# Seven block products for eight in gate and up, a down projection from scratch, and attention scores in tiles of 64 by 32

## The reference, cut to what matters

```python
h = concatenate([pad, meta, x])                        # 1024 tokens and 16 meta tokens, width 1024
proj = rmsnorm(h, norm1_g) @ w_in                      # q, k, v of attention; q, f, i, g of HGRN2
o_sb = group_rmsnorm(stick_breaking_attention(q, k, v), sb_norm_g)   # 8 heads of width 64
#   z = q @ k.T * scale; w = exp(log_sigmoid(z) + sum of log_sigmoid(-z) over later keys); w @ v
o_hg = group_rmsnorm(hgrn2_chunkwise(...), hg_norm_g) * silu(hg_g)
h = h + concatenate([o_sb, o_hg]) @ w_out
u2 = rmsnorm(h, norm2_g)                               # 1024 x 1024
h = h + (silu(u2 @ w_gate) * (u2 @ w_up)) @ w_down     # w_gate, w_up: 1024 x 2816, w_down: 2816 x 1024
return rmsnorm(h, final_norm_g)
```

## Time and profile before

| | us |
|---|---|
| median of 3 runs | 1439.6 (1439.37 to 1439.84) |
| the profiled execution: time | 1441.7 |
| the profiled execution: span of the core | 1439.7 |
| PE busy in the span | 1382.0 |
| DVE busy | 738.8 |
| ACT busy | 439.2 |
| GpSimd (POOL) busy | 20.2 |

### The profile page before, as it was taken

One profiled execution on the slowest core, in us unless ns is written; L12 is line 12 of the kernel. 1 busy time (PEld: TensorE's weight loads), 2 busy tenths in 40 slices (PEclk: granted clock), 3 DMA queues, 4 the chain that ended last, 5 costly groups with the idle time before them and its releaser, 6 DMA issues.

```text
span 1439.7 us, 22130 instructions
## 1 busy us (share of the span) xinstructions
PE 1382.0 (96%) x9404; PEld 1165.2 (81%) x9404; DVE 738.8 (51%) x1180; ACT 439.2 (31%) x768; POOL 20.2 (1%) x48
## 2 busy tenths in 40 slices
PE   6999999998999999699999999999999999999998
PEld 5898989887677776499987888888888888888886
DVE  6476677763776565822633515253342525152447
ACT  6323322223665556810522211111111211121113
POOL 3000000000000000010000000000000000000000
PEclk9999999999999999999999999999999999999999
DMA  6211111110010000041021102020201102020202
GB/s 192 59 31 30 31 31 50 31 41 1 1 60 2 31 2 30 2 161 60 30 74 59 59 30 88 0 88 18 70 29 58 58 29 85 3 87 0 88 0 117
DMA packets 61199, 68.86 MB, mean 48 GB/s; under 512 B 1584, under 2 KB 54832, under 8 KB 61120
## 3 DMA queue, kind: packets, MB, share of 16 engines
q1 hardware_dynamic: 59408, 61.94, 13.2%
q0 software_dynamic: 1712, 5.78, 1.1%
HBM read 63.51 MB, written 4.19 MB: 47 GB/s over the span
## 4 chain that ended last, share of the span: by engine, by line
PE 92%; ACT 4%; DVE 2%; issue 1%; DMA 0%; ACTq 0%; DVEq 0%; POOLq 0%
PE ps L269 19%; PE ps L271 18%; PE ps L270 18%; PE ps L1552 17%; PE ps L945 3%; PE ps L281 2%; PE ps L282 2%; PE ps L283 2%; PE ps L909 2%; PE ps L551 2%; PE ps L925 2%; PE ps L386 1%; ACT bv L505 1%; PE ps L542 1%; ACT a_hi L1020 0%
## 5 line engine op out<-in xcount | busy, mean ns | idle before, releaser
L269 PE MATMUL ps<-a_hi,w_hi 128*128 128x512 f32 (+2 forms) x960 | 358.5, 373 | 8.9 <-DVE a_lo L378 2.9
L270 PE MATMUL ps<-a_lo,w_hi 128*128 128x512 f32 (+2 forms) x960 | 350.1, 365 | 0.0
L271 PE MATMUL ps<-a_hi,w_lo 128*128 128x512 f32 (+2 forms) x960 | 349.9, 364 | 0.0
L269 PEld LDWEIGHTS ps<-a_hi,w_hi 128*128 128x128 f32 x960 | 181.8, 189 | 37.0 <-DVE a_lo L378 3.3
L271 PEld LDWEIGHTS ps<-a_hi,w_lo 128*128 128x128 f32 x960 | 181.7, 189 | 23.3
L270 PEld LDWEIGHTS ps<-a_lo,w_hi 128*128 128x128 f32 x960 | 182.2, 190 | 22.2
L1396 DVE TENSOR_TENSOR silu<-silu,ps 128x512 f32<-128x512 f32 x44 | 30.2, 687 | 319.8 <-ACT silu L1281 319.8
L1408 DVE TENSOR_TENSOR h_res<-h_res,ps 128x512 f32<-128x512 f32 x176 | 116.2, 684 | 48.1 <-PE ps L1552 47.9
L1281 ACT ACTIVATE silu<-ps 128x512 f32<-128x512 f32 x44 | 26.3, 597 | 338.1 <-PE ps L271 338.1
L269 PE MATMUL ps<-a_hi,d_hi 128*128 128x512 f32 x320 | 124.5, 389 | 0.0
L270 PE MATMUL ps<-a_lo,d_hi 128*128 128x512 f32 x320 | 124.5, 389 | 0.0
(11 more groups left out here) (193 smaller groups left out, 1901.7 us busy)
## 6 DMA issues: line engine op xcount, KB each, us to landing
w_raw<-in_w_in_dram SPq DMA_DIRECT2D x24, 512.0 KB
w_raw<-in_w_gate_dram SPq DMA_DIRECT2D x11, 1024.0 KB, 5.1
w_raw<-in_w_up_dram SPq DMA_DIRECT2D x11, 1024.0 KB, 5.1
w_raw<-in_w_down_dram SPq DMA_DIRECT2D x11, 1024.0 KB, 4.8
mixed<-in_x_dram SPq DMA_DIRECT2D x8, 512.0 KB, 7.3
w_raw<-in_w_out_dram SPq DMA_DIRECT2D x4, 1024.0 KB
h_res<-in_x_dram POOLq DMA_DIRECT2D x8, 512.0 KB, 7.5
out_dram<-h_sq SPq DMA_DIRECT2D x8, 512.0 KB, 2.6
```

The source lines that it names most:

```text
L269: nc.tensor.matmul(psum, wh, ah, start=k == 0, stop=False)
L270: nc.tensor.matmul(psum, wh, al, start=False, stop=False)
L271: last = nc.tensor.matmul(psum, wl, ah, start=False, stop=k == KT - 1)
```

## The change

**Gate and up.** The unit of work is now one matrix and 128-wide column pairs: 22 column blocks n (even: gate, odd: up), each 1024 x 256 of weights against the 1024 tokens, seen as a 2 x 2 grid of blocks (rows of the weight in halves, columns in halves, tokens in halves). Instead of eight block products of 4 steps each, seven are made (P1 to P7, 12 matmuls of 512 columns each) from sums of blocks. The sums of the tokens' blocks are made once, in the second norm, in pairs of token tiles t and t + 4 (`PAIRED`, `pair_high`, `pair_sums`, remainders on GpSimd). The sums of weights are made for every n on DVE (`weight_sums`, `weight_sum4`), each block is split on its own (`block_high` on ACT, `block_low` on DVE) into a ring of 10. The results are combined partly in PSUM and partly by copies on ACT (`hold_*`) and additions on DVE (`c11`, `c12`, `c22`), then gate and up meet in `gate_sigmoid` and `weigh_f`.

**Down.** silu(gate) times up goes to a DRAM scratch `f_spill`, the residual to `h_spill`. When gate and up are through, the down projection runs for one half of the tokens after the other, 8 banks held over all 22 row tiles of w_down; each tile of f (256 KB) and of w_down (512 KB) is loaded, rounded and split again, w_down twice in all. The number of matmuls is the same, 1056 of 512 columns; the additions to the residual are 16 in place of 176.

**Scores.** Each head's 64 by 128 matmul is four of 64 by 32.

```diff
+PRODUCTS = [("P1", 0), ("P2", 0), ("P1", 1), ("P2", 1), ("P5", 0), ("P6", 0), ("P5", 1), ("P7", 0), ("P6", 1),
+            ("P4", 0), ("P3", 0), ("P7", 1)]
+for _n in range(2, CHUNKS_GU):
+    PRODUCTS += [("P1", _n), ("P4", _n - 1), ("P3", _n - 1), ("P5", _n), ("P6", _n), ("P2", _n), ("P7", _n)]
...
-                for par in range(2):
-                    rows = slice(64 * par, 64 * par + 64)
-                    last = nc.tensor.matmul(bank(2 * par + n % 2, w), bq[rows, kv, b * P:(b + 1) * P],
-                                            bf[rows, kv, lo:hi], start=True, stop=hi < width)
+                for q in QUARTERS:
+                    for par in range(2):
+                        rows = slice(64 * par, 64 * par + 64)
+                        last = nc.tensor.matmul(bank(2 * par + n % 2, w)[q],
+                                                bq[rows, kv, b * P + q.start:b * P + q.stop],
+                                                bf[rows, kv, lo:hi], start=True, stop=hi < width)
...
+                for n in range(2, CHUNKS_GU):                      # SP
+                    sp.wait_ge(block_lo.sem, block_lo.done(NO["P3", n - 2] + 1))
+                    load_raw(n)
+                    if n % 2:
+                        store_f(n - 2)
+                for w in weighed:
+                    sp.wait_ge(w.sem, w.done(CHUNKS_GU - 1))
+                load_down(0)
+                load_down(1)
+                store_f(CHUNKS_GU - 1)
+                sp.wait_ge(block_lo.sem, block_lo.done(len(PRODUCTS)))
+                load_down(2)
+                load_down(3)
+                sp.wait_ge(product_done.sem, product_done.done(len(PRODUCTS)))
                 for t in range(TT):
+                    sp.wait_ge(x_came[t].sem, 32)
+                    sp.dma_start(h_back[t], h_spill[t * P:(t + 1) * P, :]).then_inc(x_came[t].sem, 16)
...
+                for i in range(TT):                                # ACT
+                    stats(i)
+                    if i >= 3 and i % 2:
+                        pair_high((i - 3) // 2)
+                pair_high(3)
...
+                for i, t in enumerate(PAIRED):                     # DVE
+                    add(3, i, t)
+                    if i:
+                        scale(i - 1)
+                    if i == 2:
+                        block_low(0)
+                        block_low(1)
+                    if i >= 3 and i % 2:
+                        pair_sums((i - 3) // 2)
+                scale(TT - 1)
+                pair_sums(3)
...
+                def second_transposes(i):                          # PE
+                    s = i % 2
+                    pe.wait_ge(n2_normed.sem, n2_normed.done(i + 1))
+                    if i >= 2:
+                        pe.wait_ge(t_ready.sem, t_ready.done(4 * (i // 2)))
+                    for k in range(KT):
+                        last = nc.tensor.transpose(bank(2 * s + k // 4)[:, (k % 4) * P:(k % 4) * P + P],
+                                                   h_norm[:, s, k * P:(k + 1) * P], ident[:])
+                    last.then_inc(n2_turned.sem, 1)
...
+                for n in range(2, CHUNKS_GU):
+                    p1(n)
+                    p4(n - 1)
+                    p3(n - 1)
+                    p5(n)
+                    p6(n)
+                    p2(n)
+                    p7(n)
```

More of the change, by code:

```diff
@@ L1135, in _ @@
                 load_chunk(sp, ("O", 3))
[L1137 to L1159, removed]
@@ L1169, in _ @@
+                for t in range(4, TT):
+                    store_out(t)
+                for st in stored:
+                    sp.wait_ge(st.sem, 16 * TT // 2)
             @blk.gpsimd
@@ L1256, in _ @@
                 high_chunk(act, ("O", 3), (o_proj, 2 * TT))
[L1258 to L1261, removed]
-                    nc.scalar.activation((slot or ffn_slot(c))[0], w_raw[:], ACT.Copy)\
-                        .then_inc(high[c].sem, 1)
-                split("g", 0, (o_proj, 3 * TT), ffn_slot("g", True))
@@ L1370, in _ @@
+                for c in range(3):
                     for t in range(TT):
-                        add(c, t)
+                        add(c, t, t)
                         if c == 0 and t == 0:
@@ new lines, in _, with down_add @@
+                n = CHUNKS_GU - 1
+                weigh_f(n, 0)
+                c22(n)
+                f_low(1)
+                down_low(1)
+                weigh_f(n, 3)
+                weigh_f(n, 2)
+                c12(n)
+                weigh_f(n, 1)
+                def down_add(g):
+                    t, half = g // 2, g % 2
+                    dve.wait_ge(dn_done.sem, dn_done.done(g + 1))
+                    if half == 0:
+                        dve.wait_ge(x_came[t].sem, 48)
+                    h = h_back[t][:, X_PARTS[half]]
+                    nc.vector.tensor_tensor(h, h, bank(DOWN_BANKS[g % TT]), ALU.add).then_inc(dn_add.sem, 1)
@@ L1540, in down @@
-                def down(j, par, weights=ffn_slot("d")):
-                    dh, dl = weights
-                    pe.wait_ge(low["d"].sem, low["d"].done(j + 1))
-                    pe.wait_ge(f_low.sem, f_low.done(4 * j + 4))
-                    for g in range(2 * TT):
-                        t, half = g // 2, g % 2
-                        if not (isinstance(j, int) and j == 0 and g < 4):
-                            pe.wait_ge(dn_add.sem, dn_add.done(16 * j + (g - 3)))
-                        for f in range(2):
-                            w = slice(f * D + half * HALF, f * D + (half + 1) * HALF)
-                            a = TOKEN_TILES[t]
-                            for m, (fa, dw) in enumerate(((f_hi, dh), (f_hi, dl), (f_lo, dh))):
-                                last = nc.tensor.matmul(bank(4 + g % 4), fa[:, par, f, a], dw[:, w],
-                                                        start=f == 0 and m == 0, stop=f == 1 and m == 2)
-                        last.then_inc(dn_done.sem, 1)
@@ new lines, in _, with product @@
+                second_transposes(TT - 1)
+                def product(kind, n, start):
+                    m = NO[kind, n]
+                    x, y, z = SETS[n % 2]
+                    wh, wl = ring(m)
+                    yh, yl = tokens[kind]
+                    psum = bank({"P1": x, "P2": y, "P3": z, "P4": x, "P5": z, "P6": x, "P7": x}[kind])
+                    pe.wait_ge(block_lo.sem, block_lo.done(m + 1))
+                    for k in range(UNIT):
+                        c = slice(k * P, (k + 1) * P)
+                        nc.tensor.matmul(psum, wh[:, c], yh[:, k], start=start and k == 0, stop=False,
+                                         skip_group_check=not start)
+                        nc.tensor.matmul(psum, wh[:, c], yl[:, k], start=False, stop=False, skip_group_check=not start)
+                        last = nc.tensor.matmul(psum, wl[:, c], yh[:, k], start=False, stop=k == UNIT - 1,
+                                                skip_group_check=not start)
+                    last.then_inc(product_done.sem, 1)
```

771 lines of the change are left out of this document (570 added, 201 removed).

## The result

The change makes the kernel faster, by less than forecast: 1415.1 us (four runs, 1414.1 to 1416.3) against 1439.7 us for the kernel before beside it. The ratio is 0.983, with a 95% interval of 0.9815 to 0.984: 24.7 us gained where 38.2 had been forecast. The profiled spans say the same: 1439.7 and 1414.6 us, 25.1 apart. The time lies in the range of 1390 to 1422.

The account below looks back on a forecast made before the run. PE was taken as the bound, busy 96% of the span. Matmuls and a wait -61.3, norm +18.1, clock +4, passage +3, scores -2 make -38.2 us: 1439.7 to 1401 us, range 1390 to 1422 (8 in 10).

Parts of the forecast that it names:

- Fewer matmuls, 59.8 us: Gate and up: 1848 matmuls in place of 2112, 264 fewer at 0.2267 us each, saving 59.8 us.
- 0 for the loop: Loop over the 22 blocks: other engines' work stays hidden beside PE, so it adds 0 us.
- rival 1: Loop not hidden: a hand-over comes 1 us late in every block, 22 us more, 1423 us; chance 10%.
- The norm's idle time, 18.1 us: Second norm: PE waits for the token sums of the pairs, 18.1 us in all, 15 to 23.
- The clock, 4 us: Behind the second norm's waits PE's clock falls to 1.2 GHz, costing 4 us, 0 to 6.8.
- The passage, 3 us: From the last gate/up block to down: PE waits for loads queued behind stores and residual, 3 us, 0 to 10.
- Scores, 2 us: Attention scores: 0.05 us off each of 42 groups where PE paces, saving 2 us.
- Rivals 2 and 3: Scores: column tiles overlap by twos only, 24 us lost, 6%; or stream one after the other, 71 us lost, 5%.
- Rival 4: Scores: each added instruction costs its own start, 5.6 us, 1409 us; chance 4%.
- Down: hidden, as forecast,: Down projection: 1056 matmuls as before, with DVE, ACT and load work hidden beside PE.
- Rival 5: Residual loads and tiles queue worse than rates say, or instructions come late: 12 us, not 3, 1410 us; chance 7%.
- The 19.2 us: Second norm's cost if GpSimd's remainders hold up DVE's scaling of the last tile by up to 1.1 us.

Follow-up runs that it names:

- e9: The changed kernel with the fifth product of every block done twice, 264 matmuls more: 1470.0 us, ratio 1.0205.
- e8: The changed kernel with column groups 2 and 3 of the output projection in turn: 1396.3 us, ratio 0.969.
- e7: The changed kernel with unread matmuls filling PE's idle time ahead of the transposes of tiles 2, 4 and 6: 1407.2 us, ratio 0.9774.
- e3: The changed kernel with the residual's eight loads one by one behind tiles 8 to 15: 1408.4 us, ratio 0.9784.
- e4: The changed kernel with the residual's loads late and tiles 2 and 3 loaded ahead of the last store of f: 1405.9 us, ratio 0.9764.
- e12: The changed kernel with column groups in turn, residual late, tiles 2 and 3 early, 16 unread matmuls, and two last-block ACT copies moved ahead: 1389.4 us.
- e2: The changed kernel with each head's scores as one matmul of 64 by 128 again: 1413.4 us, ratio 0.9822.
- e6: The changed kernel with ACT's roundings of a pair put ahead of the statistics of one more tile: 1408.0 us, ratio 0.978.
- e5: The kernel before with only the scores changed, to tiles of 64 by 32: 1438.1 us, ratio 0.9988.
- e11: The changed kernel with column groups in turn, residual late, tiles 2 and 3 early, and 16 unread matmuls ahead of tile 6's transposes: 1390.0 us.

## Why the prediction was right in kind and 13 us off

1. **Fewer matmuls, 59.8 us: right.** e9 puts the same number back and pays 57.8 us in that stretch, the rest being a wait that they cover. The loop shows no idle time, so "0 for the loop" stands and rival 1 falls.
2. **The norm's idle time, 18.1 us: right.** Forecast 3.8, 4.1, 7.0, 0.7, 2.5; measured 4.24, 4.23, 7.45, none, 2.60, 18.5 in all. e8, which gives PE other groups meanwhile, takes 10.5 of it away. GpSimd's remainders take 1.27 us, near the 1.13 that I had taken; the last sum waits on none of them.
3. **The clock, 4 us: too small.** The norm was to take 48.1 + 4 = 52.1 us; it takes 54.0, and the first products behind it lose 1.7 more. 3.6 us over in all, a little of it (0.4) idle time. With 30.0 us of work and 18.5 of waits the clock has 5.5 us of the 54.0, 7.2 with the products behind: more than my upper end of 6.8. I had taken 4, from one spell; four gaps brought three spells and a fourth behind the first product. e7 shows the cause, and that 3.2 of the 5.5 come back when the gaps are filled.
4. **The passage, 3 us: the step that failed.** The estimate was that "they and two tiles take 14.5 us", from the rate of 394 GB/s, against 17 us of work on PE. Measured, it is 19.1 us from the first residual load (1166.12) to the landing of the fifth tile (1185.20), and 2.5 more to its first product, 21.5 in all. PE had work for 15.5 of them and not 17. DMA in that time (columns as above, the rate last):

```profile
1164.00:1172.00 8.00, 6.46 (x29) 5.03 (x27) 1.36 (x2) 2.21 (x3) 0.00 (x0) 1.00 0.89 272
1172.00:1185.00 13.00, 11.17 (x48) 8.93 (x48) 2.81 (x4) 1.69 (x2) 0.00 (x0) 1.00 1.03 409
```

The rate held once the queue was full (409 GB/s), but was 272 while SP was still issuing, which takes it 5 us for the eight residual loads (1166.12 to 1171.05). The larger part is the bytes: 1166 to 1185 us moved 374 GB/s, 7.1 MB, where the sum had 5.7. The third and fourth tile, asked for just ahead, were still coming, and tiles behind the fifth were issued before it landed; how the 1.4 MB divide between them is open. The third tile was to come "just in time"; it came 2.2 us late. The copy on ACT that the last block waits for (1.7) was in no term, and the lower clock behind the last gap (1.7) in the clock's term only for the norm. Together 9.4 us. e3 and e4 remove all but the wait for the copy and show the queue as the cause; e12 removes that wait. Idle time counts from a matmul's modelled end; by distances of starts the passage costs 10.2 us (670.0 us from the first product to the last matmul, 658.1 for 2903 distances of 0.2267, 1.7 of the rest behind the first product). Reckoned so, the five other profiles with this queue order (e2, e6 to e9) have 7.1 to 9.9 us.
5. **Scores, 2 us: right in size, hidden in this profile.** A group saves 0.04 us and not 0.05, but 49 of the 56 start ahead of 569 us, where PE paces, and not 42, since the last pair's first ones are made ahead. e5 has 1.6; in the changed kernel's profile a spell of the lower clock leaves 0.3 ahead of the projection. Rivals 2 and 3, 24 and 71 us, fall: four column tiles of 64 by 32 with 512 columns run side by side. Rival 4 falls too: 12 more instructions made the group 0.04 us shorter. The some 60 cycles for each matmul that TensorEngine Tiling in the Trainium skill, Instruction Overhead, gives would have been an estimated 12.6 us; the rows of this kernel do not show them.
6. **Down: hidden, as forecast,** from the fifth tile on: 206 of 206 us. The tail is 7.4 us, not 6.8.

The terms miss by 3.6 (clock and norm), 7.2 (passage, 10.2 less 3), 2.1 (scores, with the first three column groups) and 0.6 (tail): 13.5 us, for the 13.1 between 1401.5 and 1414.6. All of them miss on the same side; nothing cancelled. Rival 5, "queue worse than rates say", was the nearest, at 1410 and 7%: it was given a chance that its own argument, a load behind 4.2 MB in one queue, should have made much larger.

## What to carry to other kernels

When a change removes work from a full engine, the gain per instruction is safe, and the loss sits where phases meet: list there each load's place in its queue with everything that is still to come ahead of it, and the time that it takes to issue them. A gap of several us on PE can be paid twice, once idle and once at the lower clock behind it (here the one of 3.8 us at the passage was, those of 1.7 and 2.2 were not). Filling it with real work of the neighbouring phase is best (13.9 us in e8). Unread matmuls gave 3.2 us of the norm in e7 and nothing of it in e11, where the chain on the other engines ended no sooner. A term of 2 us can be read only against the scatter of the same stretch in several profiles.

## What the runs showed of the hardware

**GpSimd and DVE shut each other out, in pieces.** The scaling on DVE (two inputs in SBUF) beside GpSimd's remainders; these are the same two engines of the changed kernel in order of time, DVE first:

```profile
702.47 0.68 DVE L1648 TENSOR_TENSOR tmp<-ps,tmp 128x512 f32<-128x512 f32 x1
...
703.59 2.10 DVE L1623 SCALAR_TENSOR_TENSOR h_norm<-h_res,small,gain 128x1024 f32<-128x1024 f32 x1
```

```profile
703.33 3.50 POOL L1312 TENSOR_TENSOR t_lo<-tmp,t_hi 128x512 fp32r<-128x512 f32 x2
...
704.56 2.26 POOL L1312 TENSOR_TENSOR t_lo<-tmp,t_hi 128x512 fp32r<-128x512 f32 x1
```

The scaling takes 2.10 us where it takes 1.28 alone. The GpSimd operation that is at work when it starts runs from 703.33 for some 1.27 us, the usual length, to 704.6; the scaling waits for the most of that. The next one, started at 704.56, takes 2.26, so it waits until the scaling ends at 705.69. DVE's sum of one input in PSUM and one in SBUF, beside GpSimd too, keeps its 0.68. This agrees with what SBUF — State Buffer in the Trainium skill, Who interferes with whom, says of a DVE instruction with two SBUF inputs and a GpSimd one that reads SBUF. Its price here is nothing: it hits tiles whose transposes come later, and the last tile's scaling ran in 1.29, while the GpSimd operation beside it took 2.35. The 19.2 us that I had worked out by the rule did not come.

**One load behind many.** 512 KB of `w_down` land in 5.2 us in the median and took 13.6 when eight loads of 512 KB had been issued in the 5 us before, while 409 GB/s moved in 1172 to 1185 us.

**Spells of the lower clock move.** In attention they fall at other places in other executions (the granted clock of 340 to 360 us is 0.83 in two profiles with the new scores and 1.00 in nine), and with the same instructions on PE the output projection starts at 607.5 to 610.8 us.
